# Attention scores from 64 partitions of queries and keys, chosen by the head's parity, in place of 128 with half of the keys zero

## The reference

```python
HEAD_DIM = 64; A_HEADS = B_HEADS = 8; A_KV_HEADS = B_KV_HEADS = 2; IDX_HEADS = 8; IDX_DIM = 64
# group A (swa_with_sinks)
s = jnp.einsum('bnqhgd,bnkhd->bnhgqk', qb, kk).astype(jnp.float32) * (D ** -0.5)
p = jax.nn.softmax(jnp.concatenate([s, sink], -1), axis=-1)[..., :-1].astype(v.dtype)
# group B (dsa_sparse_attention)
rel = jax.nn.relu(jnp.einsum('bqhd,bsd->bqhs', qib, ki).astype(jnp.float32))   # indexer
_, sel = lax.top_k(score, topk)
s = jnp.einsum('bqhgd,bqnhd->bqhgn', qg, ks).astype(jnp.float32) * (D ** -0.5)
```

## Time and profile before

| | us |
|---|---|
| median of 3 runs (1373.6 to 1376.31) | 1374.47 |
| the profiled execution's own time | 1378.29 |
| its span | 1376.5 |
| TensorE busy | 1275.7 (93%) |
| VectorE busy | 824.1 (60%) |
| ScalarE busy | 503.2 (37%) |
| GpSimd busy | 278.1 (20%) |

### The profile page before, as it was taken

One profiled execution on the slowest core, in us unless ns is written; L12 is line 12 of the kernel. 1 busy time (PEld: TensorE's weight loads), 2 busy tenths in 40 slices (PEclk: granted clock), 3 DMA queues, 4 the chain that ended last, 5 costly groups with the idle time before them and its releaser, 6 DMA issues.

```text
span 1376.5 us, 18454 instructions
## 1 busy us (share of the span) xinstructions
PE 1275.7 (93%) x6392; PEld 1052.7 (76%) x6392; DVE 824.1 (60%) x1444; ACT 503.2 (37%) x1011; POOL 278.1 (20%) x287
## 2 busy tenths in 40 slices
PE   1798997999999999999999989899999999999996
PEld 1686785788788778888778778777888877888785
DVE  6667889757777756433176688874733345333337
ACT  0444566615333211222134556672433321123210
POOL 1084135711111100000003455661000000000001
PEclk9899999999999999999999999999999999999998
DMA  8553112242787824323124220012223223232211
GB/s 322 206 193 108 62 47 67 88 138 83 275 272 261 269 75 170 107 95 104 46 77 125 80 72 1 15 49 76 78 96 103 91 78 121 92 107 91 93 44 62
DMA packets 44272, 156.17 MB, mean 113 GB/s; under 512 B 5808, under 2 KB 5808, under 8 KB 44208
## 3 DMA queue, kind: packets, MB, share of 16 engines
q1 hardware_dynamic: 30528, 109.07, 23.4%
q0 software_dynamic: 12672, 46.14, 10.2%
q10 hardware_dynamic: 1008, 0.12, 0.1%
HBM read 153.21 MB, written 2.10 MB: 113 GB/s over the span
## 4 chain that ended last, share of the span: by engine, by line
PE 73%; DVE 14%; issue 4%; ACT 4%; POOL 3%; DMA 2%; SPq 0%; DVEq 0%; ACTq 0%; POOLq 0%
PE bank L536 21%; PE bank L537 21%; PE bank L538 21%; PE bank L800 2%; DVE w_lo L1297 2%; PE bank L767 2%; DVE scores L1425 2%; PE bank L746 1%; DMA ada_w<-in_w_ada 1%; DVE top L1417 1%; DMA w_raw<-in_weights 1%; PE bank L778 1%; DVE ada_acc L1320 1%; DVE xs L1527 1%; DVE pq L1464 1%
## 5 line engine op out<-in xcount | busy, mean ns | idle before, releaser
L536 PE MATMUL bank<-hT_hi,w_hi 128*128 128x512 f32 (+1 forms) x768 | 287.5, 374 | 2.2 <-issue 1.5
L537 PE MATMUL bank<-hT_lo,w_hi 128*128 128x512 f32 (+1 forms) x768 | 286.2, 373 | 0.0
L538 PE MATMUL bank<-hT_hi,w_lo 128*128 128x512 f32 (+1 forms) x768 | 286.0, 372 | 0.0
L1678 DVE TENSOR_TENSOR w_lo<-w_raw,w_hi 128x1024 fp32r<-128x1024 f32 x88 | 107.8, 1225 | 145.6 <-ACT w_hi L1208 145.6
L1052 ACT ACTIVATE w_hi<-w_raw 128x1024 fp32r<-128x1024 f32 x96 | 100.6, 1062 | 230.9 <-PE bank L538 227.5
L536 PE MATMUL bank<-w_hi,hT_hi 128*128 128x512 f32 (+2 forms) x448 | 172.4, 385 | 13.5 <-DVE hT_lo L1382 6.5
L536 PEld LDWEIGHTS bank<-hT_hi,w_hi 128*128 128x128 f32 x768 | 145.2, 189 | 28.2 <-issue 2.3
L1297 DVE TENSOR_TENSOR w_lo<-w_raw,w_hi 128x1024 fp32r<-128x1024 f32 x88 | 115.5, 1326 | 84.1 <-ACT w_hi L1052 80.7
L538 PE MATMUL bank<-w_hi,hT_lo 128*128 128x512 f32 (+2 forms) x448 | 165.7, 370 | 0.0
L537 PE MATMUL bank<-w_lo,hT_hi 128*128 128x512 f32 (+2 forms) x448 | 165.7, 370 | 0.0
L538 PEld LDWEIGHTS bank<-hT_hi,w_lo 128*128 128x128 f32 x768 | 145.2, 189 | 25.4
(11 more groups left out here) (143 smaller groups left out, 1915.6 us busy)
## 6 DMA issues: line engine op xcount, KB each, us to landing
w_raw<-in_weights SPq DMA_DIRECT2D x184, 512.0 KB, 3.4
ada_w<-in_w_ada POOLq DMA_DIRECT2D x80, 512.0 KB, 5.0
ada_w<-in_w_ada SPq DMA_DIRECT2D x16, 512.0 KB, 5.3
xs<-in_x SPq DMA_DIRECT2D x4, 512.0 KB, 9.6
g_row<-in_ln_row POOLq DMA_DIRECT2D x4, 512.0 KB, 5.5
b_row<-in_ln_row POOLq DMA_DIRECT2D x4, 512.0 KB, 6.2
trunk_out<-xs SPq DMA_DIRECT2D x8, 256.0 KB, 2.0
modb<-in_b_ada ACTq DMA_DIRECT2D x1, 48.0 KB, 3.7
```

The costliest lines, as they stand in the source:

```text
L536: pe.matmul(dst, a_hi, b_hi, start=first, stop=False)
L537: pe.matmul(dst, a_hi, b_lo, start=False, stop=False)
L538: return pe.matmul(dst, a_lo, b_hi, start=False, stop=last)
L1678: nc.vector.tensor_tensor(w_lo[:, s, :], w_raw[:, s, :], w_hi[:, s, :].bitcast(F32), ALU.subtract).then_inc(lo_ready, 1)
```

## The change

`kT` loses its axis of key heads: key head 0 stays on partitions 0 to 63 and key head 1 on 64 to 127 of one block, as they come from the transposes. GpSimd's two fills with zeros in each layer go, with their semaphore. ScalarE copies the keys in one instruction of 128 partitions where it had two of 64. A score multiplies the 64 partitions of its head's half, of queries and of keys.

```diff
--- before.py
+++ after.py
@@ -163,7 +163,7 @@
             kiT = sb("kiT", [P, SEQ], on=att)
 
 
-            kT = sb("kT", [P, 2, KV_HEADS, SEQ], on=att)
+            kT = sb("kT", [P, 2, SEQ], on=att)
             scores = sb("scores", [P, SC_W], on=att)
             pT = sb("pT", [P, PT_RING, 512], on=att)
 
@@ -202,7 +202,6 @@
         h_hi = sem("h_hi")
         h_lo = sem("h_lo")
         proj_evac = sem("proj_evac")
-        keys_zeroed = sem("keys_zeroed")
         y_normed = sem("y_normed")
         y_squared = sem("y_squared")
         roped = sem("roped")
@@ -480,11 +479,6 @@
                     rope(l, 0, t)
                     if l == 0:
                         ada_fetch(3 * KD + t + 1)
-                pool.wait_ge(roped, at_roped(l, 0, T - 1))
-                for g in range(KV_HEADS):
-                    other = slice((1 - g) * HD, (2 - g) * HD)
-                    nc.gpsimd.memset(kT[other, :, g, :], 0.0).then_inc(keys_zeroed, 1)
-                    pool.wait_ge(keys_zeroed, 2 * l + g + 1)
                 if l == 0:
                     ada_fetch(ASIDE_FROM + RING)
                     pool.wait_ge(small_in, 16 * 6)
@@ -761,11 +755,10 @@
                     pe.wait_ge(proj_evac, at_chunk(l, 4, T - 1))
                 if kind == "B" and h == 0:
                     pe.wait_ge(qk_ready, at_chunk(l, 4, t))
-                if n == 0:
-                    pe.wait_ge(keys_zeroed, 2 * (l + 1))
                 a = int(kind == "A")
-                pe.matmul(s_bank(n)[:, 0:hi - lo], qT[:, a, h // 2, t * P:(t + 1) * P],
-                          kT[:, a, h % 2, lo:hi], start=True, stop=True).then_inc(scored, 1)
+                half = slice((h % 2) * HD, (h % 2 + 1) * HD)
+                pe.matmul(s_bank(n)[:, 0:hi - lo], qT[half, a, h // 2, t * P:(t + 1) * P],
+                          kT[half, a, lo:hi], start=True, stop=True).then_inc(scored, 1)
 
             def transpose_p(l, u, h):
                 lo, hi = keys_of(UNITS[u])
@@ -1118,10 +1111,8 @@
                 act.wait_ge(qk_transposed, at_chunk(l, c, T - 1))
                 if c == 1:
                     nc.scalar.activation(kiT[:], bank[4][:], ACT.Copy).then_inc(qk_ready, 1)
-                for g in range(KV_HEADS):
-                    half = slice(g * HD, (g + 1) * HD)
-                    nc.scalar.activation(kT[half, c // 2, g, :], bank[5 if c == 1 else 0][half, :], ACT.Copy)\
-                        .then_inc(qk_ready, 1 if (c, g) == (1, 0) else 2)
+                nc.scalar.activation(kT[:, c // 2, :], bank[5 if c == 1 else 0][:], ACT.Copy)\
+                    .then_inc(qk_ready, 3 if c == 1 else 4)
 
             def relu(l, i, h):
                 act.wait_ge(idx_scored, 24 * l + 8 * i + h + 1)
```

## The result

| | before | changed |
|---|---|---|
| median, us | 1374.86 (1373.6 to 1376.31, 4 runs) | 1413.0 (1401.58 to 1427.1, 4 runs) |
| profiled execution: time, span, clock | 1378.29, 1376.5, 0.977 | 1403.92, 1401.9, 0.969 |
| TensorE busy | 1275.7 | 1319.5 |

The changed kernel is slower: the ratio is 1.0252, with an interval from 1.0204 to 1.0301. The runs of before lie within 3 us of each other, those of the changed kernel within 26, and they go with the granted clock: 1401.58 us at 0.973, 1403.92 at 0.969, 1422.08 at 0.955, 1427.1 at 0.952. So there are two questions: what makes every run slower, and what spreads them.

What follows compares the result with a forecast made beforehand. TensorE was taken as the bound in steps 8 to 34 and after 54, VectorE in steps 0 to 7. Seams of 28.3 us less 1.2 for the copy gave 27 on 1374.5: 1401.5 us, range 1382 to 1417.

Steps and rivals of the forecast that it cites:

- A pass on 64 partitions streams no faster: Loop scores: streaming time of the 256 score passes unchanged, since 64 partitions only allow a neighbour at the same time.
- Two seams of 0.2 us: Around every loop score: changing from 128 partitions to 64 and back costs TensorE 0.40 us, 25 us a layer if unhidden.
- C and D: Attention loop steps 35 to 46 and 47 to 54: seams add 1.5 and 1.0 us in first layer, 1.5 and 2.0 in second.
- E: Loop's rest after step 54, with last transposes and values, TensorE full: seams add 2.5 and 2.8 us in the two layers.
- A: Attention loop steps 0 to 7, VectorE the bound: seams add 0.5 us in each layer.
- B: Attention loop steps 8 to 34, TensorE the bound: seams add 7.5 us in first layer, 8.5 in second.
- The copy: ScalarE's key copy ahead of the loop: one instead of two brings the first score 0.6 us earlier, 1.2 in all.
- The fills: GpSimd's 1.96 us of zero fills in each layer: removing them gains nothing, as 16 us of idle time follows.
- The clock rival: Seams as holes lower the granted clock in steps 8 to 34, each 5 us costing 2.5 more; +40 or over; chance 0.10.
- Absorbed: Rival: other engines run ahead and seams fill all TensorE's holes in the loop; +3 to +15, say 1384 us; chance 0.17.
- Concurrent passes: Rival: a score's two passes, or score and neighbour, run side by side in the loop; 1360 us; chance 0.03.
- Seams that cost nothing: Rival: the indexer block's price comes from format change, so loop seams are free and only the copy is left; 1373.3; chance 0.06.

## Why the prediction was right, and where it was not

The direction and the range held (1382 to 1417; measured 1413.0). The forecast of 1401.5 stands 11.5 us low, and its sum was made of other parts than the time: seams on 64 partitions slow the loop, as forecast, but less than forecast, and the granted clock, which was not in the sum, made up the rest. That the median lies in the range is in part luck, since the two errors offset each other; two of the four runs (1422.08 and 1427.1) lie above it.

- *A pass on 64 partitions streams no faster.* Right: in the indexer's block of the kernel before, passes on the same half after the first follow each other by 0.21 to 0.22 us at 256 columns, as on 128 partitions; in the changed loop a score's two passes, with what the seams add, take 0.62 us against 0.43.
- *Two seams of 0.2 us.* Right in kind, 0.35 us for both where 0.40 was taken from the indexer's block: 0.20 up to the score's second pass and 0.15 behind it. The seams are shown by the pitches and by the experiments that put them in one stage at a time.
- *The steps.* The cut between C and D in the earlier trace rows stands at the mask of head 46, so C has 11 steps and D 9; and E has 9 (55 to 63), not 8. At 0.40 us a seam pair none of this moves a stage by more than 0.4 us.
- *A.* 0.5 us forecast in each layer. Measured 0.1 in the first; 1.3 in the second, with the clock at 0.85 there against 0.91 in the earlier trace rows.
- *B.* 7.5 and 8.5 us forecast, 4.8 and 7.0 measured (4.7 and 7.4 where C and D had none). Too high: 27 seams of 0.35 are 9.5, and the true holes, which busy time hides, took more than the 2.3 and 1.6 us of the earlier trace rows; I had said that they would be larger and gave them too little (9.5 less 4.8 and 7.0 leaves 4.7 and 2.5 us hidden). Why the first layer hides more than the second isn't settled; VectorE has 4.4 us more work there.
- *C and D.* 2.5 and 3.5 us forecast. Measured 0.1 in the first layer of the changed kernel: the holes hide all of them. In the second 12.0, with the clock at 0.64 and 0.71. This is the term that failed, on both sides: the seams' own length, charged to the ring's latencies, is nearly nothing, and the lower clock, which comes with them here, wasn't in the sum.
- *E.* 2.5 and 2.8 forecast; 1.3 and 2.4 in the kernel with no seams in steps 35 to 54, 1.3 and 4.2 in the changed one.
- So the seams' term of 28.3 us measured 16 to 20, and the clock's term, which had no place in the likeliest case, 18 at the median (changed kernel less the one without seams in steps 35 to 54).
- *The copy.* 1.2 us forecast. In the chain 0.6 us of copy is gone, in the time of the kernel with that alone nothing can be told (ratio 1.0018, 0.999 to 1.0046). *The fills.* Nothing, as forecast.
- *The clock rival.* It had 0.10 and looked in the wrong place: it asked whether the clock would fall in B, where a step streams without pause, and B is at 1.00 in every profile. It falls in C or D, where the earlier trace rows show TensorE busy for 13.21 of 17.80 us in C. Its price was put at 2.5 us for each fall of 5; but a fall there lasted 30.8 us in the changed kernel and 41 in the one with seams in these steps alone. Falls as such come there without seams too, and end after 3 to 7 us.
- *Absorbed*: half true, for C and D. *Concurrent passes*: not in the changed kernel; once scores are neighbours, true in full of a bit over half of the pairs. *Seams that cost nothing*: false.

## What to carry to other kernels

A matmul on half of the partitions is no cheaper by itself than one on all of them; it pays only beside a neighbour on the other half, and every change between 128 and 64 partitions took some 0.2 us (0.35 for both around a score), as the next weights are then not loaded under the pass ahead. Zero halves, which look like waste, were the cheap way here: half-height scores came out 2.5% slower singly and equal in pairs. And before calling a cost on TensorE hidden in its holes, look at the granted clock of that stage, in more than one execution: an edit there can turn falls of 3 to 7 us into falls of 20 to 48, far more than its own time, and a spread of the runs that follows the clock is the sign.

## What the runs showed of the hardware

At the lower level TensorE had almost no idle time left (busy for 29.99 of 30.80 us at 0.50 in the changed kernel, for 40.22 of 41.00 and 40.12 of 40.90 in the kernel with seams in steps 35 to 54 alone), and still the clock stayed down until the last single score on 64 partitions, or for some 30 us of them. A stage that is busy without pause by the profile's measure is thus no sign that the clock will come back. Nor does the busy share ahead tell that it will fall: TensorE was busy for 9.82 of the 10.70 us before the fall in the changed kernel, and for 29.70 of 39.00 us in C and D of the kernel before, where none came.

Open are two things. Whether a pass on 64 partitions does less to bring the clock back than one on 128 was not tried apart from the seams. And why the fall comes in one layer of one execution and in the other of another isn't known.
